# Second block's two norm statistics: every row of squares added on GpSimd, the weighted squares made by ScalarE

## The chip, the cores and the metric
The kernel runs on one core of one Trainium2 chip. The metric is the device time of one launch in microseconds (us), the median of several runs. TensorE, VectorE, ScalarE, GpSimd and SyncE each work through their own instruction list and wait for each other through semaphores. The profile calls them PE (PEld for its weight loads), DVE, ACT, POOL and SP.

## The reference, cut to what matters
Two transformer blocks run one after the other on 256 tokens of width 1024. The first one ends in a norm, the second one begins with one:

```
x = x + 0.5 * ml[8] * swiglu(modulate(rms_norm(x, norm3_g), ml[6], ml[7]), ffn2_w_in, ffn2_w_out)
x = rms_norm(x, final_g)            # end of the first block
h = rms_norm_2(x, norm_mix)         # start of the second block
proj = h @ w_in                     # queries, keys, values, gates, pooled rows
```

With r the reciprocal root of mean(x*x) + eps, the second norm needs the mean of (x * r * final_g) squared. Both means can be had from the x ahead of the first norm: one is the sum of x*x over the 1024 features, the other the sum of (x * final_g) squared. So one statistics step serves both norms.

## The kernel before, in words
Everything is kept with features on the 128 partitions: x is 8 tiles (kc = 0 to 7) of 128 features by 256 tokens. Weights stream in as "units" of 128 x 2048 numbers (1 MB, L378 on SP). ScalarE copies each half of a unit to w_hi in the rounded fp32r format (L524), VectorE forms the rest w_lo = raw - w_hi (L991), and TensorE multiplies high by high, high by low and low by high (L1799 to L1801): for 256 tokens, 8 tiles kc x 2 output tiles x 3 = 48 products in a unit. There are two buffers of each, so unit k+2 is loaded when both halves of w_lo of unit k are made, and it is split when TensorE is through with unit k.

The stage around the change is the end of the first block's second swiglu and the start of the second block. The last four units of the swiglu (`out_parts`, called for i = 0 to 3) give two tiles of x each (m = 0, 2, 4, 6). For each pair the order on VectorE is: add the unit's result to x (L1114), make w_lo of half 1 of the unit two ahead (L991), make x_lo of both tiles (L1161), make w_lo of half 0 of the unit three ahead (L991). The order on ScalarE is: split half 1 of the unit two ahead, x_hi of both tiles (L584), split half 0 of the unit three ahead, squares of both tiles into sq (L588). With i = 1 a table load (L549) stands ahead of this. Each engine goes through this list in order.

TensorE then runs the unit `kcvc` (the second block's first, L2062) on x_hi and x_lo as they come: tile kc waits for that tile's x_lo (`xl_ready`), and the unit's start waits until the swiglu's last but one unit has been added to x (`drained`). Within that unit `mix_ready` puts `mix_stat(kc - 2)`: two products per tile kc of the squares with a two-column operand `sq_gain` (a column of ones and a column of final_g squared), which sum both statistics into ps_a (L2053). The last two tiles' products stand behind the unit. Then come eight products for the gate logits (L2069), and the next unit, inside which at kc = 3 the result of the statistics is spread over partitions (`spread(3, 4)`, L1747).

Behind `stat_done` VectorE makes two variances (L1446 to L1450), ScalarE the root (L782), VectorE half 1 of the w_lo of unit `kcvc` + 2 and the reciprocal (L1054). SP waits for `stat_done` as well, ahead of two 1 MB transfers of late compression weights into sq (L421) and of the later unit loads. GpSimd waits for it ahead of two memsets (L498, L500).

All other norms of the kernel use another way: GpSimd adds the squares of tiles 1 to 5 onto tile 0 (`sums`, L454; `SUMMED` is 6), and TensorE multiplies tiles 6 and 7 and the sum with a column of ones (`stat_rows`, L1730). Each add waits for the one before it.

Of the kernel before, what the change touches and what calls it, by code (L numbers as in the profile page):

```python
# [8 lines left out]
ACT = mybir.ActivationFunctionType  # L9
ALU = mybir.AluOpType  # L10
# [3 lines left out]
P = 128  # L14
D = 1024
KD = D // P
# [3 lines left out]
TT = S // P  # L20
EPS = 1e-6
SUMMED = KD - 2


D_FF = 2816
# [79 lines left out]
def program(nc, a, out):  # L105
    with ExitStack() as ctx:
# [22 lines left out]
        vec = sb("vec", [P, V_END])  # L129
        late_w = sb("late_w", [P, L_END])  # L130
        gg = sb("gg", [P, KD])
        sq_gain = sb("sq_gain", [P, KD, 2])
        sc_pad = sb("sc_pad", [P, KD, MOD_ROWS])
        one_col = sb("one_col", [P, 2, MOD_ROWS])
        turned = sb("turned", [P, MOD_COLS])
# [309 lines left out]
        @block.gpsimd  # L445
        def _(pool):
            def sums(n, width):

                made = n if n < 3 else n - 1
                for kc in range(1, SUMMED):  # L450
                    pool.wait_ge(sq_ready, KD * n + kc + 1)
                    if kc > 1:
                        pool.wait_ge(sq_sums, (SUMMED - 1) * made + kc - 1)
                    pool.tensor_tensor(sq[:, 0, 0:width], sq[:, 0, 0:width], sq[:, kc, 0:width], ALU.add).then_inc(sq_sums, 1)  # L454

            sums(0, NB)
            sums(1, NB)

            for g in range(HKV):
                with pool.Fori(0, 2) as p:  # L460
                    for j in range(2):
                        k = FIRST["conv"] + 4 * g + j
                        if j == 0:
                            pool.wait_ge(drained, FIRST["gates"] + 2 + GROUP * (g + 1))
                        pool.wait_ge(halves_done, 4 * p + 2 * k + 2)
                        pool.tensor_copy(q_cur[:, j, :], q_rows[:, 2 * p + (4 * g + j), :]).then_inc(qcur_ready, 1)
            sums(2, S)

            def pool_group(i):

                w = POOLS[i]
                first = 7 * i
                pool.wait_ge(pool_copied, i // 2 + 1)
                if i:
                    pool.wait_ge(pooled_ready, i)
                pool.tensor_tensor(p_pad[:, PAD:PAD + S], pooled[:, i, :], r_mix, ALU.mult).then_inc(pool_steps, 1)
                pool.wait_ge(pool_steps, first + 1)
                width, step = 1, 0
                bufs = (s1[:, 0, :], s1[:, 1, :])
                while width < w:  # L480
                    dst, lo = bufs[step % 2], 2 * width - 1
                    prev = p_pad if step == 0 else bufs[(step - 1) % 2]
                    ins = pool.tensor_tensor(dst[:, lo:PAD + S], prev[:, lo:PAD + S], prev[:, lo - width:PAD + S - width], ALU.add)
                    step += 1
                    ins.then_inc(pool_steps, 1)
                    pool.wait_ge(pool_steps, first + 1 + step)
                    width *= 2
                sums_w, res = bufs[(step - 1) % 2], bufs[step % 2]
                cnt = cst[:, K_CNT + i * PAD:K_CNT + (i + 1) * PAD]
                pool.tensor_tensor(res[:, 0:PAD], sums_w[:, PAD:2 * PAD], cnt, ALU.mult)  # L490
                pool.tensor_scalar(res[:, PAD:S], sums_w[:, 2 * PAD:PAD + S], 1.0 / w, None, ALU.mult)\
                    .then_inc(pool_steps, 6 - step)
                pool.wait_ge(pool_steps, first + 7)
                pool.tensor_tensor(pooled[:, i, :], res[:, 0:S], p_pad[:, PAD:PAD + S], ALU.subtract).then_inc(pooled_ready, 1)

            pool.wait_ge(sq_sums, 3 * (SUMMED - 1))
            pool.wait_ge(stat_done, 4)
            pool.memset(h_lo[:, 6:8, :].bitcast(F32), 0.0).then_inc(k2_zeroed, 1)  # L498
            pool.wait_ge(k2_zeroed, 1)
            pool.memset(kc_st.bitcast(F32), 0.0).then_inc(k2_zeroed, 1)  # L500
            for r in range(4):
                pool.wait_ge(qk_done, HQ + 2 * r + 1)
                if r == 0:
                    pool.wait_ge(hid_done, 2)
                    pool.wait_ge(rmix_ready, 1)
                    pool.wait_ge(gt_ready, 1)
                pool_group(r)
            sums(4, S)
            sums(5, S)
# [3 lines left out]
        def _(act):  # L513
# [59 lines left out]
                        act.wait_ge(drained, 2 * pr + (k + 3))  # L573
                    act.activation(sq[:, m + t, 0:n], x[:, m + t, 0:n], ACT.Square).then_inc(sq_ready, 1)

            def out_parts(k, m, dst, gain, early):

                split(0, k + 2, 1)
                for t in range(2):
                    if t == 0:  # L580
                        act.wait_ge(first_added, early)
                    else:
                        act.wait_ge(drained, k + 3)
                    act.activation(dst[:, m + t, :], x[:, m + t, 0:S], ACT.Identity, scale=gain(m + t)).then_inc(xh_ready, 1)  # L584
                if m < KD - 2:
                    split(0, k + 3, 0)
                for t in range(2):
                    act.activation(sq[:, m + t, 0:S], x[:, m + t, 0:S], ACT.Square).then_inc(sq_ready, 1)  # L588

            def out_step(pr, k0, i, n, early, last=True, more=True):  # L590

# [68 lines left out]
            def swiglu_wide(base, count):  # L660
                def hidden(pr, k, c, chunks):
                    for m in range(chunks):
                        copy_lo(pr, k + m, m % 2)
                        split(pr, k + m + 2, 1)
                        act.wait_ge(halves_summed, c - count + m + 1)
                        act.activation(s1[:, m % 2, 0:S], s1[:, m % 2, 0:S], ACT.Silu).then_inc(silu_done, 1)
                        act.wait_ge(prod_done, c + m + 1)
                        act.activation(h_hi[:, m, 0:S], t1[:, m % 2, 0:S], ACT.Copy).then_inc(hh_done, 1)
                        split_ahead(pr, k + m)

                split(0, base + 2, 0)
                for s in range(2):
                    hidden(s * 6, base, s * 8 + count, SLABS[0])
                    for i in range(4):
                        split(s * 6, base + SLABS[0] + i + 2, 1)
                        split_ahead(s * 6, base + SLABS[0] + i)
                hidden(0, base + 24, count + 16, SLABS[2])
                for i in range(4):
                    if i == 1:
                        prepare_root()  # L680
                    out_parts(base + 24 + SLABS[2] + i, 2 * i, x_hi[:, :, S:NB], lambda m: gg[:, m:m + 1], 3 + i)


            swiglu(FIRST["ffn1"], 0, NB)
# [286 lines left out]
        def _(dve):  # L971
# [211 lines left out]
                splits(0, 1)  # L1183

            norm_lo(0, 0, NB, modulated(0, 1), 0, between=shift)

            dve.memset(sq_gain[:, :, 0], 1.0)
            dve.tensor_tensor(sq_gain[:, :, 1], vec[:, V_F1:V_F1 + KD], vec[:, V_F1:V_F1 + KD], ALU.mult)

            def swiglu(base, count, n, i):  # L1190
                def gate(m, s):
# [524 lines left out]
        def _(pe):  # L1716
# [2 lines left out]

            def stat_rows(n, tiles, rows, first, last):  # L1720

                made = n if n < 3 else n - 1
                for kc in rows:
                    if kc == 0:
                        pe.wait_ge(sq_sums, (SUMMED - 1) * (made + 1))
                    else:
                        pe.wait_ge(sq_ready, KD * n + kc + 1)
                    for t in range(tiles):

                        ins = pe.matmul(ps_a[:, 3, t:t + 1], sq[:, kc, t * P:(t + 1) * P], ones[:, 0:1],  # L1730
                                        start=(kc == first and t == 0), stop=(kc == last and t == tiles - 1))
                if kc == last:
                    ins.then_inc(stat_done, 1)

            def stat(n, tiles):
                stat_rows(n, tiles, (*range(SUMMED, KD), 0), SUMMED, 0)

            def stat_sums(n, tiles):
                stat_rows(n, tiles, (0,), 0, KD - 1)
# [307 lines left out]

            k = FIRST["kcvc"]

            def mix_stat(kc):  # L2050
                pe.wait_ge(sq_ready, KD * 3 + kc + 1)
                for t in range(TT):
                    ins = pe.matmul(ps_a[:, 3, t:t + TT + 1:TT], sq[:, kc, t * P:(t + 1) * P], sq_gain[:, kc, :],  # L2053
                                    start=(kc == 0 and t == 0), stop=(kc == KD - 1 and t == TT - 1))
                return ins

            def mix_ready(kc):
                pe.wait_ge(xl_ready, 8 * 3 + kc + 1)
                if kc >= 2:
                    mix_stat(kc - 2)  # L2060

            unit(0, k, mix_in, ready=mix_ready)  # L2062
            mix_stat(KD - 2)
            mix_stat(KD - 1).then_inc(stat_done, 1)

            pe.wait_ge(wg_ready, 1)
            for kc in range(KD):
                g = kc % 4
                ins = pe.matmul(ps_a[32 * g:32 * g + 32, 1, 0:S], wg_gain[:, kc * 3 * H2:kc * 3 * H2 + 32], x[:, kc, 0:S],  # L2069
                                start=(kc < 4), stop=(kc >= KD - 4))  # L2070
            ins.then_inc(gt_done, 1)

            def spread_within(kc):
                if kc == 3:
# [350 lines left out]
```

## Time and profile before

| what | value |
|---|---|
| median of 3 runs | 1256.49 us (1254.65 to 1256.58) |
| the profiled execution's own time | 1256.76 us |
| its span in the trace | 1255.0 us |
| granted TensorE clock, mean | 0.996 |
| PE busy | 1239.7 us, 99% |
| DVE busy | 888.6 us, 71% |
| ACT busy | 574.9 us, 46% |
| POOL busy | 55.0 us, 4% |

Times are counted from the start of the span. The stage of the change lies at 866 to 900 us. Matmul records overlap, since TensorE is pipelined: what one costs is the distance from its start to the next one's start. An fp32 product that isn't in the rounded format shows as two records. A "releaser" in square brackets is what ended the idle time ahead of the instruction.

### The profile page before, as it was taken

To read this page: it belongs to the slowest core of one execution; us is meant where nothing else is said; L and a number is where in the kernel's file an instruction comes from. 1 tells how busy PE (TensorE), PEld (TensorE's weight loads), DVE (VectorE), ACT (ScalarE), POOL (GpSimd) and SP (SyncE) were. 2 spreads that over 40 slices of the span, in tenths; PEclk is the share of its full clock that TensorE was granted. 3 is DMA by queue.
4 is the path that set the end of the run, shared out by engine and by line. 5 is a ranking of instruction groups with operands and counts; after the bars stand their busy time and mean duration, and the time that the engine had idled before them with its cause. 6 is when DMAs were issued, how large, how long until landed. Compare 5 with 4: busy or idle time off the path is not lost.

```text
span 1255.0 us, 20607 instructions
## 1 busy us (share of the span) xinstructions
PE 1239.7 (99%) x7778; PEld 1093.1 (87%) x7778; DVE 888.6 (71%) x1395; ACT 574.9 (46%) x880; POOL 55.0 (4%) x65
## 2 busy tenths in 40 slices
PE   8999999999999999999999999999999999999998
PEld 7788888888888799988999888889999999888887
DVE  3887777777754765777666676767769977666765
ACT  3632123221234446554444654556475566554553
POOL 2000000000002000100001000000011301000001
PEclk8999999999999999999999999999999999999999
DMA  9565544455413234422445465544633334455542
GB/s 388 227 237 201 201 184 167 186 201 201 160 62 115 75 144 150 168 101 102 168 167 199 146 245 181 199 174 166 233 135 115 121 131 172 168 187 202 181 168 101
DMA packets 31826, 214.22 MB, mean 171 GB/s; under 512 B 3472, under 2 KB 4752, under 8 KB 7056
## 3 DMA queue, kind: packets, MB, share of 16 engines
q1 hardware_dynamic: 31184, 211.83, 46.0%
q10 hardware_dynamic: 576, 1.48, 0.3%
q8 instruction: 46, 0.75, 0.2%
q14 instruction: 20, 0.16, 0.0%
HBM read 212.24 MB, written 1.05 MB: 170 GB/s over the span
## 4 chain that ended last, share of the span: by engine, by line
PE 95%; DVE 2%; DMA 1%; issue 1%; ACT 0%; SPq 0%; DVEq 0%
PE ps_u L1801 28%; PE ps_u L1799 20%; PE ps_u L1800 19%; PE ps_u L1796 18%; PE ps_a L1718 1%; DMA scr<-in_mods 1%; PE ps_a L2001 1%; PE ps_a L1986 1%; PE ps_a L1764 1%; PE ps_a L1775 1%; PE ps_a L2190 1%; PE ps_a L1753 0%; PE ps_a L1730 0%; PE ps_a L1747 0%; DVE w_lo L991 0%
## 5 line engine op out<-in xcount | busy, mean ns | idle before, releaser
L524 ACT ACTIVATE w_hi<-raw 128x1024 fp32r<-128x1024 f32 x322 | 338.9, 1056 | 313.8 <-PE ps_u L1801 216.0
L991 DVE TENSOR_TENSOR w_lo<-raw,w_hi 128x1024 fp32r<-128x1024 f32 x322 | 393.4, 1223 | 121.0 <-ACT w_hi L524 120.5
L1801 PE MATMUL ps_u<-x_hi,w_lo 128*128 128x256 f32 (+1 forms) x1488 | 460.7, 310 | 0.0
L1799 PE MATMUL ps_u<-x_hi,w_hi 128*128 128x256 f32 (+1 forms) x1136 | 370.7, 326 | 2.5 <-DVE x_lo L1077 1.3
L1800 PE MATMUL ps_u<-x_lo,w_hi 128*128 128x256 f32 (+1 forms) x1072 | 344.2, 321 | 0.0
L1801 PEld LDWEIGHTS ps_u<-x_hi,w_lo 128*128 128x128 f32 x1488 | 282.6, 190 | 15.3
L1801 PE MATMUL ps_u<-h_hi,w_lo 128*128 128x256 f32 (+1 forms) x800 | 244.2, 305 | 0.0
L1799 PEld LDWEIGHTS ps_u<-x_hi,w_hi 128*128 128x128 f32 x1136 | 216.0, 190 | 25.9 <-issue 8.4
L1800 PEld LDWEIGHTS ps_u<-x_lo,w_hi 128*128 128x128 f32 x1072 | 203.9, 190 | 15.3 <-issue 0.5
L1801 PEld LDWEIGHTS ps_u<-h_hi,w_lo 128*128 128x128 f32 x800 | 151.6, 190 | 7.0
L1799 PE MATMUL ps_u<-h_hi,w_hi 128*128 128x256 f32 (+1 forms) x432 | 141.7, 328 | 0.4 <-DVE h_hi L1218 0.4
L1796 PE MATMUL ps_u<-h_hi,w_hi 128*128 128x512 f32 x368 | 129.5, 396 | 0.0
L1796 PE MATMUL ps_u<-x_hi,w_hi 128*128 128x512 f32 x352 | 122.7, 392 | 0.4 <-DVE x_hi L1077 0.4
L1800 PE MATMUL ps_u<-h_lo,w_hi 128*128 128x256 f32 (+1 forms) x368 | 122.9, 334 | 0.0
L1796 PE MATMUL ps_u<-x_lo,w_hi 128*128 128x512 f32 x256 | 90.8, 399 | 0.0
L1799 PEld LDWEIGHTS ps_u<-h_hi,w_hi 128*128 128x128 f32 x432 | 82.1, 190 | 8.4 <-issue 0.8
L1796 PEld LDWEIGHTS ps_u<-h_hi,w_hi 128*128 128x128 f32 x368 | 69.0, 188 | 16.5
L1796 PEld LDWEIGHTS ps_u<-x_hi,w_hi 128*128 128x128 f32 x352 | 65.8, 187 | 15.8 <-issue 1.0
L1800 PEld LDWEIGHTS ps_u<-h_lo,w_hi 128*128 128x128 f32 x368 | 69.9, 190 | 6.9
L1801 PE MATMUL ps_u<-x_lo,w_lo 128*128 128x256 f32 x256 | 71.8, 280 | 0.0
L1024 DVE SCALAR_TENSOR_TENSOR sq<-scr,sc_pad,sq 128x1024 f32<-128x1024 f32 x56 | 68.1, 1279 | 0.0
L1124 DVE TENSOR_TENSOR s<-ps_u,s 128x512 f32<-128x512 f32 x38 | 26.3, 692 | 49.2 <-ACT s L622 48.8
(293 smaller groups left out, 1216.0 us busy)
## 6 DMA issues: line engine op xcount, KB each, us to landing
raw<-in_stream SPq DMA_DIRECT2D x153, 1024.0 KB, 4.8
wide_scr<-in_mods SPq DMA_DIRECT2D x18, 1024.0 KB, 6.9
scr<-in_mods SPq DMA_DIRECT2D x18, 1024.0 KB, 6.9
raw<-in_stream SPq DMA_DIRECT2D x8, 768.0 KB, 4.0
x<-in_tokens SPq DMA_DIRECT2D x2, 1024.0 KB, 6.5
wide_scr<-in_cmp_w SPq DMA_DIRECT2D x8, 256.0 KB, 5.1
sq<-in_cmp_w SPq DMA_DIRECT2D x2, 1024.0 KB, 7.3
out<-x SPq DMA_DIRECT2D x4, 256.0 KB, 2.2
```

The lines of the kernel that those rows point to most:

```text
L524: act.activation(w_hi[:, k % 2, cols], raw[:, k % 2, cols], ACT.Copy).then_inc(h_ready, 1)
L991: dve.tensor_tensor(w_lo[:, k % 2, cols], raw[:, k % 2, cols], w_hi[:, k % 2, cols].bitcast(F32), ALU.subtract).then_inc(l_ready, 1)
L1024: ins = dve.scalar_tensor_tensor(total_v, w[:, kc, :], by, total_v, ALU.mult, ALU.add)
L1124: dve.tensor_tensor(both, ps_u[:, b:b + 2, 0:S], both, ALU.add).then_inc(halves_summed, 1)
L1718: return pe.transpose(dst, src, ident[0:n, 0:n])
L1764: ins = pe.matmul(ps_a[rows, b, 0:MOD_COLS], sc_pad[:, 2 * quarter + kc, :], mod_slots[slot][:, lo:lo + MOD_COLS], start=(quarter == 0 and ...
L1775: ins = pe.matmul(ps_a[rows, MOD_BANKS[c], 0:MOD_COLS], one_col[:, v, :], mod_sums[:, c % 2, v, g * MOD_COLS:(g + 1) * MOD_COLS], start=(v ...
L1796: pe.matmul(ps_u[:, 2 * b + t, :], wh, both, start=(kc == 0), stop=False)
L1799: pe.matmul(dst, wh, xh, start=(kc == 0), stop=False)
L1800: pe.matmul(dst, wh, xl, start=False, stop=False)
L1801: ins = pe.matmul(dst, wl, xh, start=False, stop=(kc == span - 1))
L1986: ins = pe.matmul(ps_a[:, qt, :], q_cur[:, j, qt * P:(qt + 1) * P], k_all[:, g, :], start=True, stop=True)
```

## The change
GpSimd gets a fourth turn, `sums(3, NB)`, over all eight tiles and over 512 columns: columns 0 to 255 hold the squares of x, columns 256 to 511 the squares of x times final_g. ScalarE makes the second half with one more Square per tile, with final_g as its scale. TensorE no longer has `mix_stat`; it multiplies the finished sum by a column of ones, four column blocks of 128 tokens, behind the gate logits' products. `sq_gain` and its two VectorE instructions at the kernel's start go. The table `ADDED` says how many tiles GpSimd adds in each norm, and the semaphore targets follow from it.

```diff
+ADDED = (SUMMED, SUMMED, SUMMED, KD, KD, SUMMED)
@@ gpsimd, sums(n, width)
-                made = n if n < 3 else n - 1
-                for kc in range(1, SUMMED):
+                made = sum(ADDED[0:n]) - n
+                for kc in range(1, ADDED[n]):
                     pool.wait_ge(sq_ready, KD * n + kc + 1)
                     if kc > 1:
-                        pool.wait_ge(sq_sums, (SUMMED - 1) * made + kc - 1)
+                        pool.wait_ge(sq_sums, made + kc - 1)
@@
             sums(2, S)
+            sums(3, NB)
@@ scalar, out_parts(k, m, dst, gain, early, also=None)
                 for t in range(2):
-                    act.activation(sq[:, m + t, 0:S], x[:, m + t, 0:S], ACT.Square).then_inc(sq_ready, 1)
+                    ins = act.activation(sq[:, m + t, 0:S], x[:, m + t, 0:S], ACT.Square)
+                    if also is not None:
+                        ins = act.activation(sq[:, m + t, S:NB], x[:, m + t, 0:S], ACT.Square, scale=also(m + t))
+                    ins.then_inc(sq_ready, 1)
@@ vector
-            dve.memset(sq_gain[:, :, 0], 1.0)
-            dve.tensor_tensor(sq_gain[:, :, 1], vec[:, V_F1:V_F1 + KD], vec[:, V_F1:V_F1 + KD], ALU.mult)
@@ tensor
             def stat(n, tiles):
-                stat_rows(n, tiles, (*range(SUMMED, KD), 0), SUMMED, 0)
+                stat_rows(n, tiles, (0,), 0, 0)
@@
-            def mix_stat(kc): ...
-            def mix_ready(kc): ...
-            unit(0, k, mix_in, ready=mix_ready)
-            mix_stat(KD - 2)
-            mix_stat(KD - 1).then_inc(stat_done, 1)
-
+            unit(0, k, mix_in, ready=normed(3))
             pe.wait_ge(wg_ready, 1)
             for kc in range(KD):
                 ...
             ins.then_inc(gt_done, 1)
+            stat(3, 2 * TT)
```

`stat` is also used by the norm behind the second block's attention (n = 4, `stat(4, 2)` at L2254, between the first two units of the feed-forward stage, around 1068 us). Its entry in `ADDED` is KD as well: there GpSimd now adds all eight tiles of 256 columns, and TensorE multiplies only the sum (two products) where it multiplied tiles 6, 7 and the sum (six).

## Rows read from the trace of the kernel before

**Rows 1.** Page, chain that ended last: shares of the span by engine.
```profile
PE 95%; DVE 2%; DMA 1%; issue 1%; ACT 0%; SPq 0%; DVEq 0%
```

**Rows 2.** Timeline of PE, 879 to 893 us: start, length, line, out<-in, count.
```profile
879.76 0.28 PE L1799 MATMUL ps_u<-x_hi,w_hi 128*128 128x256 f32 x1
...
881.20 0.51 PE L2053 MATMUL ps_a<-sq_gain,sq 128*128 128x2 f32 x4
...
889.04 1.07 PE L2069 MATMUL ps_a<-x,wg_gain 128*32 128x256 f32 x16
890.04 0.39 PE L1799 MATMUL ps_u<-x_hi,w_hi 128*128 128x256 f32 x1
...
892.29 1.05 PE L1747 MATMUL ps_a<-cst,rstd 128*128 128x128 f32 x8
```

**Rows 3.** Timeline of PE at the feed-forward stage's norm (n = 4).
```profile
1068.18 1.39 PE L1730 MATMUL ps_a<-ones,sq 128*128 128x1 f32 x12
1069.44 0.48 PE L1796 MATMUL ps_u<-x_lo,w_hi 128*128 128x512 f32 x1
```

**Rows 4.** Timeline of ACT, 872 to 886 us.
```profile
872.31 0.71 ACT L588 ACTIVATE sq<-x 128x256 f32<-128x256 f32 x2
...
881.82 1.06 ACT L524 ACTIVATE w_hi<-raw 128x1024 fp32r<-128x1024 f32 x1 [1.81 <-DMA raw<-in_stream]
...
884.64 0.91 ACT L584 ACTIVATE x_hi<-x,gg 128x256 fp32r<-128x256 f32 x2 [0.20 <-DVE x L1114]
885.45 0.71 ACT L588 ACTIVATE sq<-x 128x256 f32<-128x256 f32 x2
```

**Rows 5.** Groups by shape, 868 to 890 us: busy us, mean ns of one.
```profile
L584 ACT ACTIVATE x_hi<-x,gg 128x256 fp32r<-128x256 f32 x8 | 3.6, 501 | 1.1 <-DVE x L1114 1.1
...
L588 ACT ACTIVATE sq<-x 128x256 f32<-128x256 f32 x8 | 2.8, 401 | 0.0
```

**Rows 6.** Timeline of DVE, 875 to 892 us.
```profile
875.51 1.23 DVE L991 TENSOR_TENSOR w_lo<-raw,w_hi 128x1024 fp32r<-128x1024 f32 x1 [0.99 <-ACT w_hi L524]
...
878.58 0.87 DVE L1114 SCALAR_TENSOR_TENSOR x<-ps_u,gate_half,x 128x256 f32<-128x256 f32 x2
...
885.18 0.89 DVE L1161 SCALAR_TENSOR_TENSOR x_lo<-x,gg,x_hi 128x256 fp32r<-128x256 f32 x2 [0.19 <-ACT x_hi L584]
...
889.90 0.12 DVE L1446 TENSOR_SCALAR var<-ps_a 128x4 f32<-128x4 f32 x1
...
891.48 0.17 DVE L1054 RECIPROCAL rstd<-root 128x4 f32<-128x4 f32 x1
```

**Rows 7.** Timeline of SP's queue: start of a unit's load.
```profile
876.92 0.33 SPq L378 DMA_DIRECT2D raw<-in_stream  x1
```

**Rows 8.** Timeline of POOL, whole span.
```profile
7.73 6.94 POOL L454 TENSOR_TENSOR sq<-sq 128x512 f32<-128x512 f32 x5 [7.30 <-ACT sq L545]
...
388.65 2.97 POOL L454 TENSOR_TENSOR sq<-sq 128x512 f32<-128x512 f32 x2 [5.59 <-ACT sq L574]
...
940.46 0.74 POOL L494 TENSOR_TENSOR x<-s,p_pad 128x256 f32<-128x256 f32 x1
...
995.65 3.02 POOL L483 TENSOR_TENSOR s<-s 128x269 f32<-128x269 f32 x3
...
1061.36 2.43 POOL L454 TENSOR_TENSOR sq<-sq 128x256 f32<-128x256 f32 x2 [3.33 <-ACT sq L588]
```

**Rows 9.** Timeline of DVE beside three of these.
```profile
387.82 1.21 DVE L991 TENSOR_TENSOR w_lo<-raw,w_hi 128x1024 fp32r<-128x1024 f32 x1
...
940.59 0.89 DVE L1501 TENSOR_TENSOR x<-t 128x256 f32<-128x256 f32 x1
...
996.66 1.41 DVE L991 TENSOR_TENSOR w_lo<-raw,w_hi 128x1024 fp32r<-128x1024 f32 x1
```

**Rows 10.** Timeline of ACT at the norm n = 4.
```profile
1064.49 0.71 ACT L588 ACTIVATE sq<-x 128x256 f32<-128x256 f32 x2
```

**Rows 11.** Stretch: engines' busy time (count), granted PE clock, DMA share, GB/s.
```profile
16.00:18.00 2.00, 0.79 (x8) 0.48 (x11) 0.18 (x1) 0.26 (x1) 0.00 (x0) 0.61 1.02 422
```

More of the change, by code:

```diff
@@ L131, in program @@
         gg = sb("gg", [P, KD])
-        sq_gain = sb("sq_gain", [P, KD, 2])
         sc_pad = sb("sc_pad", [P, KD, MOD_ROWS])
@@ L494, in pool_group @@
                 pool.tensor_tensor(pooled[:, i, :], res[:, 0:S], p_pad[:, PAD:PAD + S], ALU.subtract).then_inc(pooled_ready, 1)
-            pool.wait_ge(sq_sums, 3 * (SUMMED - 1))
+            pool.wait_ge(sq_sums, sum(ADDED[0:4]) - 4)
             pool.wait_ge(stat_done, 4)
@@ L574, in squares, with out_parts @@
                     act.activation(sq[:, m + t, 0:n], x[:, m + t, 0:n], ACT.Square).then_inc(sq_ready, 1)
-            def out_parts(k, m, dst, gain, early):
+            def out_parts(k, m, dst, gain, early, also=None):
                 split(0, k + 2, 1)
@@ L680, in swiglu_wide @@
                         prepare_root()
-                    out_parts(base + 24 + SLABS[2] + i, 2 * i, x_hi[:, :, S:NB], lambda m: gg[:, m:m + 1], 3 + i)
+                    out_parts(base + 24 + SLABS[2] + i, 2 * i, x_hi[:, :, S:NB], lambda m: gg[:, m:m + 1], 3 + i, lambda m: vcol(V_F1, m))
             swiglu(FIRST["ffn1"], 0, NB)
@@ L1720, in stat_rows @@
             def stat_rows(n, tiles, rows, first, last):
-                made = n if n < 3 else n - 1
                 for kc in rows:
                     if kc == 0:
-                        pe.wait_ge(sq_sums, (SUMMED - 1) * (made + 1))
+                        pe.wait_ge(sq_sums, sum(ADDED[0:n + 1]) - (n + 1))
                     else:
@@ L2048, in _ @@
             k = FIRST["kcvc"]
[L2050 to L2060, printed above, removed]
-            unit(0, k, mix_in, ready=mix_ready)
-            mix_stat(KD - 2)
-            mix_stat(KD - 1).then_inc(stat_done, 1)
+            unit(0, k, mix_in, ready=normed(3))
             pe.wait_ge(wg_ready, 1)
```

## The prediction, made blind
> **What bounds the kernel now.** I read the page first. TensorE is busy 99% of the span and makes 95% of the chain that ended last [rows 1], so an edit is worth what it takes from TensorE's own list, less every wait that it puts there. The reader is to see that 71% or 46% busy VectorE and ScalarE have room on average and perhaps none in the stage of the change. So I read next the timelines of that stage, engine by engine: what TensorE spends on the statistics [rows 2], in which order ScalarE and VectorE hand over the last tiles [rows 4, 6], when the next unit's load starts [rows 7]. Last, I looked at what GpSimd's adds cost elsewhere, alone and beside VectorE [rows 8, 9].
>
> **TensorE, first norm (n = 3): saves 3.5, adds 0.84.** The unit `kcvc` starts at 879.76 [rows 2]. Between two `mix_stat` groups six products take 0.72 us, 0.12 each, so its 48 would be through at 885.52; the gate products start at 889.04 [rows 2]. The 16 products of `mix_stat` (32 records) thus cost 3.52 us. The new step has four products, 8 records. Twelve such records cost 1.26 us (1068.18 to 1069.44, [rows 3]), so 8 cost 0.84. Net on TensorE: -2.7 us, if nothing is late.
>
> **TensorE, second norm (n = 4): saves 0.84.** Six products become two, 12 records become 4: 8 x 0.105 = 0.84 us. GpSimd gets two more adds of 256 columns. Its fourth and fifth add take from 1061.36 to 1063.79 with a conflict in them [rows 8], and the squares of tiles 6 and 7 are made from 1064.49 to 1065.2 [rows 10]. Another such pair would be through at 1065.0 + 2.4 = 1067.4, before TensorE asks for the sum at 1068.18: hidden, with 0.8 us to spare. With a second conflict it would be some 0.4 us late, so this term lies between -0.4 and -0.84. I take -0.84.
>
> **ScalarE's second squares: +0.8 us per pair of tiles.** A Square with no operand for its scale takes 0.40 us and two start 0.31 apart (0.71 for two); an activation with a scale per partition takes 0.50 and two start 0.41 apart [rows 4, 5]. I take 0.4 for each of the eight new ones, 0.8 a pair (0.6 if they cost as the plain ones, 1.0 if nothing overlaps). Not all of it is hidden, since the squares stand in the middle of the list:
> - Behind the first pair's squares (872.31) come the table load and the w_hi for which VectorE waits at 875.51 [rows 4, 6]. ScalarE has no idle time in between, so that w_lo starts at 876.3. All of VectorE's list moves with it: the add of the third pair ends at 880.25 instead of 879.45 [rows 6]. The unit `kcvc` needs that bank, and started at 879.76: it starts at 880.3, +0.5 on TensorE.
> - SP's load of the unit after `kcvc` starts right behind that w_lo (876.92, [rows 7]) and lets ScalarE go on at 881.82, 4.9 later [rows 4]. It becomes 877.7 and 882.6.
> - From there ScalarE has w_hi (0.95 to the next start), four squares instead of two (1.5), w_hi (0.95), and then x_hi of the last pair: 886.0, where it was 884.64 [rows 4]. The last x_lo pair, 885.18 before [rows 6], could start at 886.5.
>
> TensorE without `mix_stat` would reach tile 6 at 880.3 + 6 x 0.72 = 884.6. So it waits there in any case: even with ScalarE as before, x_lo of tile 6 comes at 885.65. Part of the old statistics work lay in a time that TensorE would else have waited.
>
> **GpSimd's seven adds.** An add of 512 columns takes 1.27 us alone and the next starts 0.14 later: five in 6.94 [rows 8]. With squares of tiles 4 and 5 at 884.4 and 885.1, of 6 and 7 at 887.6 and 888.3, adds without any disturbance end at 890.3.
>
> They will be disturbed. At 388.65 a pair takes 2.97 instead of 2.68, while a w_lo of VectorE runs until 389.03: the add waited out that instruction [rows 8, 9]. At 940.59 VectorE's 256-column operation takes 0.89, where two of that width take 0.89 together in [rows 6], beside an add that had started 0.13 earlier [rows 8, 9]. So they take turns when VectorE has two operands in SBUF, as w_lo and x_lo do. VectorE's list between 883 and 891 is mostly these. Which of two waiting instructions comes first no row shows. Let them alternate: add 5 takes 886.3 to 887.6; x_lo of tile 6, ready to start at 886.5, takes until 888.0; add 6 until 889.3; x_lo of tile 7 until 889.7; add 7 until 891.0; then the w_lo that was due at 887. TensorE starts tile 6 at 888.05 and tile 7 at 889.75, ends the unit at 890.5, the gate products at 891.5, the new step at 892.3. The next unit started at 890.04 [rows 2]: **+2.3 us**.
>
> Behind it VectorE is one w_lo in arrears. Variances at 889.90, reciprocal at 891.48 to 891.65 [rows 6], 1.75 later; TensorE asked for it at 892.29 [rows 2], 2.25 into its unit. Now VectorE comes to the variances only at 893.3, the reciprocal is there at 895.05, TensorE asks at 894.55: **+0.5**. Together n = 3 gives +2.8.
>
> The Trainium skill, "SBUF — State Buffer", section "SBUF: two separate sides", says of the ports that VectorE and GpSimd share that they are an exclusive lock: whichever starts first has them for its whole instruction and "the other fully blocks". The two cases above agree. The row at 995.65 doesn't: three adds of 269 columns take 3.02 us, at least 0.6 more than three times the 0.74 of a lone 256-column one with gaps, though the second had begun before the w_lo at 996.66, which itself lost only 0.2 of its 1.41 [rows 8, 9]. By the rule the sum stays +2.8; by that row VectorE loses less and the adds more, which is the slow rival below.
>
> **What costs nothing.** The two instructions for `sq_gain` at the start are a few dozen columns (0 to -0.2; I take 0). SP's late weights and the unit loads behind them go out about 3 us later; two 1 MB transfers at 4.9 each [rows 4, 7] have more than a unit and a half of TensorE's time, 9 us and more, before the late weights are read. GpSimd's two memsets move 3 us; the keys that they prepare come several units later. If the late weights had less room, the wait would fall on TensorE one for one. All later work is bound by TensorE, so a delay at 892 is neither made good nor enlarged.
>
> **Sum.** +2.8 - 0.84 = +2.0 us on the profiled execution's 1256.76 us (span 1255.0 and 1.8 around it), which lies 0.3 above the median: **1258.5 us** for a median run. About 0.2%, 2.5 us, is what a measurement of this kernel can tell from no change, so this counts as no change.
>
> **The rivals.**
> - *The adds hardly disturb* (they fall between VectorE's instructions). For it: the pair at 388.65 lost only 0.3. Against: VectorE has little idle time here. Then the adds end at 890.3, the step at 891.15, +1.1 for n = 3, +0.3 in all: 1256.8.
> - *Waits are shorter than I think, TensorE keeps its saving.* ScalarE's squares fall into its waits for loads, x_lo of tile 6 comes at 885.65, the unit ends at 887.15, gate products at 888.15, the step at 889.0: -1.0, with n = 4 -1.9: 1254.6. It needs all seven adds done by 888.15, from squares made at 886.5 at the earliest: against it speaks 1.27 for each of the last adds.
> - *The other side: VectorE keeps the ports, and TensorE's clock falls.* VectorE's x_lo pair and w_lo follow without a gap from 886.45 to 888.5, add 5 runs only then, another w_lo comes between, the last add ends at 893.5, and the next unit starts at 894.35: +4.3, with n = 4 +3.5, 1260.0. TensorE would be through with the gate products at 889.4 and stand idle for over 4 us. Between 16 and 18 us the granted clock fell to 0.61 of full speed on average, that is to 1.2 GHz within the stretch, after small products and waits [rows 11]. If that happens here and 5 us of products run at 1.2 instead of 2.4 GHz, 2.5 us more: 1262.5. It is over the 2.5 us once the last add ends later than 892.55 (then the step is done at 893.4, +3.35, less 0.84), or once the clock falls on top of my own waits.
> - *The change doesn't do what it says*: the final weights' squares are also made by the scaled Square, so the work is the same; I give this nothing.
>
> **How the numbers follow.** My alternating case 0.45 (its own range 1257.2 to 1260, both sides of the bound's edge at 1259.0: a quarter of it counts as slower). The undisturbed adds 0.22, no change. The saving kept 0.08; its -1.9 is just inside the bound, and I give 0.05 to faster. The slow case 0.25. Slower: 0.25 x 0.8 + 0.45 x 0.25, about 0.31; faster 0.05; same 0.64. The range leaves out the fast rival's far end and the clock's: 1255.6 to 1262.0.
>
> **What would show it.** Right: `kcvc` starts 0.3 to 0.6 later against the unit before it; TensorE waits for x_lo of tile 6 by 1.5 to 3.5 us, and the statistics step waits for GpSimd or comes right behind its last add; w_lo, x_lo or adds longer than 1.22, 0.48 and 1.27; at n = 4 no wait, and the next unit 0.84 nearer. Wrong: if the adds all take 1.27, contention is not the term; if ScalarE's list isn't late at 876, the 0.8 per pair isn't; if the next unit starts within 0.5 of 890.0, the waits are overrated; if the granted clock leaves 1.00 near 890, the slow rival has it.

## The result and the profile after

| | before | after |
|---|---|---|
| median | 1256.53 us (6 runs, 1254.65 to 1256.97) | 1264.14 us (6 runs, 1262.60 to 1265.46) |
| profiled execution | 1256.76 us, span 1255.0 | 1264.16 us, span 1262.4 |
| granted clock, mean | 0.996 | 0.994 |

The ratio is 1.0062, with a 95% interval of 1.0049 to 1.0075: slower by 0.6%, where 1258.5 us and a range up to 1262.0 were forecast. A later measurement of the same program, against 35 runs of the kernel before, gave 1.0027 (1.0015 to 1.0038). Why one program has two such results is a question of its own below. The first four experiments ran on one chip (11 on record), this later measurement and all the others on another (6); the chip of the first measurement is not on record. On chip 11 the kernel before had a median of 1256.72 in 30 runs, on chip 6 of 1259.42 in 35.

Where the 7.4 us of the profiled execution lie comes from laying the two lists of TensorE side by side and comparing the distances between the same products. The front of the kernel is 0.5 shorter. The 480 wide products (512 columns) of the second swiglu, whose instructions the change doesn't touch, take 3.1 longer (169.74 for 166.64). From the swiglu's very last product (879.64 before, 882.30 after) to the first product of the compression's hidden layer (`hidden(0)`, L2087 before, L2073 after) it is 22.39 for 17.22, **+5.17**; this is "the stage" from here on. The feed-forward stage, with the norm n = 4, is 0.45 shorter (176.29 for 176.74). The rest agrees within 0.1.

The page's chain has less TensorE in it than the 95% of [rows 1]:
```profile
PE 92%; DVE 3%; DMA 2%; ACT 1%; issue 1%; SPq 0%; DVEq 0%; ACTq 0%
```

Now the timeline of TensorE in the stage. Everything that stands at some time of before is 2.6 later here before the change does anything, because of the longer stage ahead (+3.1) and the shorter front (-0.5); take 2.6 from a time to compare it with [rows 2].
```profile
883.13 0.39 PE L1799 MATMUL ps_u<-x_hi,w_hi 128*128 128x256 f32 x1 [0.55 <-DVE x L1118]
...
890.56 0.38 PE L1799 MATMUL ps_u<-x_hi,w_hi 128*128 128x256 f32 x1 [2.80 <-DVE x_lo L1165]
...
891.99 0.39 PE L1799 MATMUL ps_u<-x_hi,w_hi 128*128 128x256 f32 x1 [0.46 <-DVE x_lo L1165]
...
892.96 1.94 PE L2054 MATMUL ps_a<-x,wg_gain 128*32 128x256 f32 x16
894.83 1.87 PE L1730 MATMUL ps_a<-ones,sq 128*128 128x1 f32 x8
896.56 0.56 PE L1799 MATMUL ps_u<-x_hi,w_hi 128*128 128x256 f32 x1
896.92 0.41 PE L1800 MATMUL ps_u<-x_lo,w_hi 128*128 128x256 f32 x1
897.13 0.41 PE L1801 MATMUL ps_u<-x_hi,w_lo 128*128 128x256 f32 x1
...
900.12 1.05 PE L1747 MATMUL ps_a<-cst,rstd 128*128 128x128 f32 x8
```
Read it from the brackets. TensorE waits at the unit's start, then 2.80 for tile 6 and 0.46 for tile 7. There is no bracket at L1730: GpSimd's sum was never late. Behind the waits every length doubles: the gate products take 1.94 where they took 1.07, and the next unit's products come 0.21 apart and not 0.12. The stretches (start and end, then busy time and count of PE, PEld, DVE, ACT and POOL, granted clock, DMA share, GB/s) give the reason:
```profile
885.00:890.00 5.00, 2.76 (x23) 2.56 (x21) 4.21 (x6) 4.71 (x10) 3.38 (x3) 1.00 0.65 210
890.00:895.00 5.00, 3.98 (x29) 2.30 (x30) 5.00 (x4) 2.93 (x5) 2.79 (x3) 0.77 0.01 2
895.00:900.00 5.00, 5.00 (x25) 5.00 (x26) 2.82 (x8) 0.21 (x1) 1.10 (x2) 0.54 0.89 339
900.00:905.00 5.00, 5.00 (x49) 4.78 (x51) 3.61 (x9) 2.35 (x2) 0.00 (x0) 1.00 1.02 428
```
The clock was at 2.4 GHz, TensorE was busy for only 2.76 of 5 us, and then 1.2 GHz was granted, from 892.7 to 899.6 by the profile's record of it. TensorE has 25 products in the 5 us where the next 5 us hold 49.

VectorE's timeline holds what TensorE waited for:
```profile
884.43 1.91 DVE L1165 SCALAR_TENSOR_TENSOR x_lo<-x,gg,x_hi 128x256 fp32r<-128x256 f32 x2
...
889.14 2.79 DVE L1165 SCALAR_TENSOR_TENSOR x_lo<-x,gg,x_hi 128x256 fp32r<-128x256 f32 x2 [0.68 <-ACT x_hi L585]
891.86 3.43 DVE L995 TENSOR_TENSOR w_lo<-raw,w_hi 128x1024 fp32r<-128x1024 f32 x2
...
896.74 0.16 DVE L1447 TENSOR_SCALAR var<-ps_a 128x4 f32<-128x4 f32 x1 [1.33 <-PE ps_a L1730]
896.93 0.87 DVE L1449 TENSOR_SCALAR var<-var 128x2 f32<-128x2 f32 x1
```
The pair of x_lo that took 0.89 in [rows 6] takes 1.91 and 2.79. The first of these overlaps the end of GpSimd's second line, the other lies inside its third:
```profile
876.72 1.30 POOL L454 TENSOR_TENSOR sq<-sq 128x512 f32<-128x512 f32 x1 [189.52 <-ACT sq L591]
881.64 4.02 POOL L454 TENSOR_TENSOR sq<-sq 128x512 f32<-128x512 f32 x2 [3.62 <-ACT sq L591]
887.13 5.94 POOL L454 TENSOR_TENSOR sq<-sq 128x512 f32<-128x512 f32 x4 [1.47 <-ACT sq L591]
896.82 0.95 POOL L499 MEMSET h_lo<- 128x1024 f32 x1 [3.75 <-PE ps_a L1730]
```
ScalarE's two squares, as groups of the stretch 868 to 893:
```profile
L591 ACT ACTIVATE sq<-x,vec 128x256 f32<-128x256 f32 x8 | 4.0, 496 | 0.0
L589 ACT ACTIVATE sq<-x 128x256 f32<-128x256 f32 x8 | 3.2, 402 | 0.0
```

### The profile page after: what moved, and what is told of

Same layout as the page of the kernel before. It is cut to its first block, busy times and chain, and to the rows that moved or that the text cites. A ratio compares the mean times of both kernels' runs of the same rounds, so it can differ in the third digit from the quotient of the medians.

```text
span 1262.4 us, 20561 instructions
## 1 busy us (share of the span) xinstructions
PE 1243.3 (98%) x7746; PEld 1092.4 (87%) x7746; DVE 894.8 (71%) x1393; ACT 578.2 (46%) x888; POOL 67.8 (5%) x74
## 4 chain that ended last, share of the span: by engine, by line
PE 92%; DVE 3%; DMA 2%; ACT 1%; issue 1%; SPq 0%; DVEq 0%; ACTq 0%
PE ps_u L1801 27%; PE ps_u L1799 19%; PE ps_u L1800 19%; PE ps_u L1796 17%; PE ps_a L1719 1%; DMA scr<-in_mods 1%; DMA raw<-in_stream 1%; PE ps_a L2001 1%; PE ps_a L1986 1%; DVE w_lo L995 1%; PE ps_a L1775 1%; PE ps_a L1764 1%; PE ps_a L1730 1%; PE ps_a L2176 1%; PE ps_a L1753 0%
## 5 line engine op out<-in xcount | busy, mean ns | idle before, releaser
L454 POOL TENSOR_TENSOR sq<-sq 128x512 f32<-128x512 f32 (+1 forms) x34 | 41.8, 1228 | 920.4 <-ACT sq L575 657.9
```

## The experiments

The theory after the result: ScalarE's extra squares make the last x_hi late, GpSimd's adds stretch VectorE's x_lo behind it, TensorE stands still for some 3 us, and its clock falls. Beside that, something that is not the change makes the stages of 512-column products longer or shorter. The rival for the last was that the new or earlier waits on GpSimd do that.

### One norm at a time: n4only and n3only

`n4only` keeps the three new pieces away from n = 3 (`mix_stat`, `sq_gain` and the plain squares are as before). Its table, beside that of the changed kernel:
```diff
-ADDED = (SUMMED, SUMMED, SUMMED, KD, KD, SUMMED)
+ADDED = (SUMMED, SUMMED, SUMMED, 1, KD, SUMMED)
```


> The kernel before with the second norm's half of the change alone: GpSimd adds all eight tiles at n = 4, the first norm stays on TensorE with its 16 products. My theory: 8 records less on TensorE, -0.84 us (12 records took 1.26), the adds hidden; 1255.7 against 1256.5. Rival: this half carries part of the +7.6 us, by conflicts of the two later adds with VectorE's w_lo, or by the slower 512-column products of the swiglu stage (step 236.6 ns instead of 230 between 710 and 866 us): then +2 to +3.

`n3only` is its complement:
```diff
-ADDED = (SUMMED, SUMMED, SUMMED, KD, KD, SUMMED)
+ADDED = (SUMMED, SUMMED, SUMMED, KD, SUMMED, SUMMED)
 def stat(n, tiles):
-    stat_rows(n, tiles, (0,), 0, 0)
+    stat_rows(n, tiles, (0,) if n == 3 else (*range(SUMMED, KD), 0), 0 if n == 3 else SUMMED, 0)
```


> The changed kernel with the second norm as before: the first norm's half of the change alone. My theory: it carries all of the loss, 1264.1 + 0.84 = 1265.0, with the granted clock at 0.5 for some 7 us near 892 and the 512-column products of the swiglu stage at a step of 236.6 ns. Rival (the two halves share the loss): 1262 or less.

`n4only`: 1256.03 us beside 1256.72, ratio 0.9994 (0.9977 to 1.0011), profiled 1253.08. `n3only`: 1263.50, ratio 1.0048 (1.0029 to 1.0067), profiled 1263.50; its stage is 21.40, +4.18, with the clock down for 3.4 us where 7 were expected. All of the loss is in n = 3. (Its ratio is worth 6.0 us and its stage 4.2; the first 480 wide products of this execution are long as well, 169.74.) In TensorE's timeline of `n4only` the twelve records of [rows 3] are four:
```profile
1068.11 0.50 PE L1730 MATMUL ps_a<-ones,sq 128*128 128x1 f32 x4
1068.47 0.48 PE L1796 MATMUL ps_u<-x_lo,w_hi 128*128 128x512 f32 x1
```
From its start to the next product it is 0.36, where it was 1.26: -0.9, and no wait.

### ScalarE's squares alone: actonly

The kernel before, with the second squares made and read by nobody (the diff is cut: `out_parts` also gets the parameter `also`, and this stage's call passes the column of final_g for it):
```diff
 for t in range(2):
-    act.activation(sq[:, m + t, 0:S], x[:, m + t, 0:S], ACT.Square).then_inc(sq_ready, 1)
+    ins = act.activation(sq[:, m + t, 0:S], x[:, m + t, 0:S], ACT.Square)
+    if also is not None:
+        ins = act.activation(sq[:, m + t, S:NB], x[:, m + t, 0:S], ACT.Square, scale=also(m + t))
+    ins.then_inc(sq_ready, 1)
```


> The kernel before plus ScalarE's eight scaled squares, which nobody reads; statistics stay on TensorE. Theory: the squares move VectorE's list by 0.8 at 876 and 1.4 at the last x_lo, but TensorE with its 3.5 us of statistics between the tiles gets to tile 6 only at 885.84, so the wait is under 1 us plus 0.5 at the unit's start: +0.5 to +1.5. Rival: the squares are hidden, under +0.3. The clock stays at 1.00 in both. Swiglu stage: if the slower products come from ScalarE's longer program they show here (236.6 ns); if from GpSimd's waiting, they stay at 230.

1257.83 us beside 1256.72, ratio 1.0013 (1.0001 to 1.0024), profiled stage 18.32, **+1.10**. TensorE's waits in 868 to 905 (what waited, for what: us in total, times, longest):
```profile
PE ps_a L2056 <- DVE x_lo L1164: 0.4, 1, 0.4
PE ps_u L1802 <- DVE x L1117: 0.2, 1, 0.2
```
So ScalarE's list costs only 1.1, in the middle of the +0.5 to +1.5 expected, while `mix_stat` still stands between the tiles: TensorE has that work to do while x_lo is on its way. In the changed kernel the same delay meets an empty TensorE.

### The pace of the wide products, first try: poolwait

```diff
 pool.wait_ge(sq_sums, 3 * (SUMMED - 1))
+pool.wait_ge(sq_ready, KD * 3 + 2)
 pool.wait_ge(stat_done, 4)
```


> The kernel before with one more wait on GpSimd: ahead of its two memsets it waits for the first pair's squares (sq_ready) and then for stat_done, so during the swiglu it stands at the semaphore that the changed kernel's adds wait for, but adds nothing. Theory: which semaphore GpSimd waits for while the products run sets their pace: step 236.6 instead of 230 ns between 710 and 866 us, +3.2 us. Rival: the pace comes from where the loops lie in the program, or from something else in the program: 230 or any other value, and 1256.5 within 0.5.

1256.69 beside 1256.72, ratio 0.9996 (0.9983 to 1.0009), stage 17.22 as before, wide products at 231.6 ns in the first stage. So what GpSimd waits for doesn't fix their pace, and the 3.2 us expected from it are not there. The theory fell. Whether it changes how often they are slow, one profile can't say.

### Is it the clock: fill

The changed kernel, with five products of no use issued ahead of tile 6, so that TensorE is not idle there:
```diff
-unit(0, k, mix_in, ready=normed(3))
+def filled(kc):
+    if kc == 6:
+        keep_busy(5)
+    pe.wait_ge(xl_ready, 8 * 3 + kc + 1)
+
+unit(0, k, mix_in, ready=filled)
```


> The changed kernel with five products of ones by cos1 into an unused bank, which nobody reads, ahead of TensorE's wait for x_lo of tile 6: 2.3 us of work in a wait of 2.8. Theory (the granted clock falls because TensorE stands idle there, and that costs 3.1 us: gate products 1.94 instead of 1.07, statistics 1.87 instead of 0.95, then 1.3 in the next unit): clock 1.00 all through 885 to 905, and 1261.0 in place of 1264.1. Rival (the clock falls from something else, or the loss is all waiting): clock low near 893 as before, 1264 or more.

1261.28 beside 1259.42, ratio 1.0019 (1.0007 to 1.0031), profiled 1256.35. TensorE's timeline, filler first:
```profile
883.87 2.32 PE L1753 MATMUL ps_a<-cst,ones 128*128 128x256 f32 x10
887.01 0.39 PE L1799 MATMUL ps_u<-x_hi,w_hi 128*128 128x256 f32 x1 [0.82 <-DVE x_lo L1165]
...
888.44 0.38 PE L1799 MATMUL ps_u<-x_hi,w_hi 128*128 128x256 f32 x1 [0.45 <-DVE x_lo L1165]
```
The stretch behind it, with the columns of the stretches above:
```profile
890.00:895.00 5.00, 4.68 (x43) 4.13 (x36) 3.85 (x9) 0.72 (x2) 1.11 (x2) 1.00 0.61 218
```
x_lo is as late as before (pairs of 1.91 and 2.79), the idle 2.8 is 0.82, the clock stays at 2.4 GHz throughout, and the stage is 19.76: +2.54 instead of +5.17. The filler does not speed x_lo up; it only keeps the clock. That it does so is shown by more than this execution. Each run's mean granted clock is on record: 0.996 to 0.998 in all twelve of `fill`, as in the kernel before (0.995 to 0.998 in 82 runs), and 0.991 to 0.997 in the twelve of the changed kernel measured beside them (`again`, below), nine of them at 0.995 or less. The times show it less well: the median of `fill` is only 0.5 us below that of `again` (1261.77), the two ratios' intervals overlap, and the 1256.35 of the profiled execution is the lowest of the twelve. So the medians do not show the 3 us expected; by stages the two profiled executions differ by 1.6.

### How much the adds take from VectorE: tinyadds

The changed kernel with adds of one column, so that it leaves the sums out and keeps every wait:
```diff
-sums(3, NB)
+sums(3, 1)
```


> The changed kernel with GpSimd's seven adds of the first norm one column wide instead of 512 (the sums are left out, so the norm's statistic is not the reference's); waits, squares and TensorE's list as in the changed kernel. Theory: the adds cost by holding the ports against VectorE (x_lo 1.91 and 2.79 us for two instead of 0.88, w_lo 3.43 for two): these go back to 0.88 and 2.35, TensorE's wait for tile 6 goes from 2.8 to some 1.7 and the one for tile 7 goes; 1.6 us less waiting, and with less idle time the clock may hold: 1259.4 (with the clock's fall 1262.5). Rival (x_lo is late by ScalarE's squares and the load alone): the wait stays at 2.5 to 2.8, 1263 to 1264.

1258.62 beside 1259.42, ratio 0.9999 (0.9985 to 1.0014), stage 18.52, +1.30. VectorE's last x_lo pair and the way to the reciprocal:
```profile
889.18 0.88 DVE L1165 SCALAR_TENSOR_TENSOR x_lo<-x,gg,x_hi 128x256 fp32r<-128x256 f32 x2 [0.68 <-ACT x_hi L585]
...
893.43 0.17 DVE L1447 TENSOR_SCALAR var<-ps_a 128x4 f32<-128x4 f32 x1
893.63 0.86 DVE L1449 TENSOR_SCALAR var<-var 128x2 f32<-128x2 f32 x1
...
895.74 0.17 DVE L1058 RECIPROCAL rstd<-root 128x4 f32<-128x4 f32 x1
```
TensorE at tile 6:
```profile
889.72 0.38 PE L1799 MATMUL ps_u<-x_hi,w_hi 128*128 128x256 f32 x1 [2.28 <-DVE x_lo L1165]
```
With nothing to take turns with, the pair is at 0.88 again and tile 7 has no wait. Tile 6 still waits 2.3, more than the 1.7 expected: what is left is ScalarE's delay and the removed statistics (how the two share it is not shown). The clock held in this execution, after 2.3 of idle time ahead of tile 6; with 2.8 to 3.0 there it fell in each of the four that show it (the changed kernel twice, `n3only`, `sixadds`). But 2.3 is not safe: two of the other runs of `tinyadds` have a mean granted clock of 0.993 and 0.994, lower than any of the 82 runs of the kernel before.

### Fewer adds, more on TensorE: sixadds

```diff
-ADDED = (SUMMED, SUMMED, SUMMED, KD, KD, SUMMED)
+ADDED = (SUMMED, SUMMED, SUMMED, SUMMED, KD, SUMMED)
 def stat(n, tiles):
-    stat_rows(n, tiles, (0,), 0, 0)
+    stat_rows(n, tiles, (*range(SUMMED, KD), 0) if n == 3 else (0,), SUMMED if n == 3 else 0, 0)
```


> The changed kernel with the first norm's sum over six tiles instead of eight: GpSimd's adds 6 and 7 go, TensorE multiplies tiles 6 and 7 as well, 12 products (24 records, 2.5 us) instead of 4 (0.84). Theory: adds 6 and 7 ran beside the last x_lo and the two w_lo behind it; without them the second x_lo and w_lo are not held, 0.5 us less waiting, 1.7 more products, but the clock falls all the same since the wait for tile 6 stays 2.8: 1264.5 to 1266. Rival: conflicts at the end are the main loss, 1262 or less.

1262.46 beside 1259.42, ratio 1.0037 (1.0017 to 1.0057), below the 1264.5 to 1266 expected; profiled 1269.14 with a stage of 27.59, +10.4. TensorE waited 3.0 for tile 6 (until 890.5), and the clock fell for 17.1 us, here from 889.5 on, with the wait not yet over:
```profile
890.00:895.00 5.00, 4.50 (x28) 3.23 (x28) 3.27 (x6) 2.88 (x5) 0.17 (x1) 0.50 0.38 103
895.00:900.00 5.00, 5.00 (x27) 4.77 (x23) 0.00 (x0) 0.00 (x0) 0.00 (x0) 0.50 0.25 107
```
Its runs lie in two groups, 1258.3 to 1263 and 1267.8 to 1269.1, and only one of the second is profiled. The mean granted clock tells them apart: 0.990 to 0.992 in the four of the second group, 0.994 to 0.996 in the six of the first. So the second group is that of the long fall.

### The changed kernel once more: again

No edit.

> The changed kernel once more, unedited, to have more runs of it beside the others on one chip. If its six runs of 1262.6 to 1265.5 are typical: 1264.1. If the pace of the 512-column products (230 or 236 ns in the profiled executions, which differs from kernel to kernel and once changed within a run) is drawn anew in each execution, and the profiled one had the slow pace in both stages: median 1262.5, runs from 1259 to 1267.

1261.77 beside 1259.42, ratio 1.0027 (1.0015 to 1.0038), profiled 1261.33. Stage 21.33, +4.11, with the waits of the first profile (3.3 for x_lo, 0.5 at the start) and a fall of the clock half as long, 3.4 us:
```profile
890.00:895.00 5.00, 4.19 (x28) 2.73 (x28) 5.00 (x4) 2.74 (x5) 2.58 (x3) 0.66 0.01 2
```
So the waits belong to the kernel, and the length of the fall to the execution; two of the twelve runs, with a mean clock of 0.997, seem to have had none.

### The kernel before, three times, and n = 4 alone: base_a to base_c, n4_again

The three of base are the kernel before, unedited; `n4_again` is `n4only`, unedited.

> The kernel before, unedited, for a second profiled execution. Theory (the pace of the 512-column products is drawn anew in each execution): the two stages of such products, 710 to 866 us and 1100 to 1240 us, run at about 230 or about 236.5 ns from start to start, in combinations that differ between executions of this one program, and the time is near 1253.4, 1256.5 or 1259.8 us as none, one or both of them are slow. Rival (the pace belongs to the program): 230 in the first stage and 236.7 in the second again, as in the first profile of this kernel.

> The kernel before once more, unedited, a third profiled execution. As for the last: by the theory of a draw at least one of the two new executions shows another combination of paces than 230 and 236.7; by the rival both show that one, and 1256.5 us.

> The kernel before, a fourth profiled execution. In each of the four, time less the extra of the slow stages (3.3 us each by the earlier profiles) should be 1253.2 within 0.7 us if the pace is all that moves this kernel's time.

> The candidate: the change at the second norm (n = 4) alone, once more, to narrow its interval. Forecast -0.84 us, a ratio of 0.9993, from eight records of 0.105 us; with this kernel's executions spread over 6 us the interval will probably be some 0.0015 wide to each side and not exclude 1. Rival (something else is lost elsewhere by the two later adds): 1.0000 or over.

| kernel before | first wide stage | second wide stage | time |
|---|---|---|---|
| first profile | 166.64 | 176.74 | 1256.76 |
| base_a | 166.64 | 176.81 | 1256.27 |
| base_b | 169.73 | 174.08 | 1256.63 |
| base_c | 166.63 | 176.82 | 1256.21 |

The wide stages are TensorE's times from the first to the last of 480 (second swiglu) and 496 (feed-forward stage) wide products. One and the same program has either the one long or the other. It can be read in any profile, from the mean length of such a product (groups by shape, 720 to 860 us). In the first profile of before:
```profile
L1796 PE MATMUL ps_u<-x_hi,w_hi 128*128 128x512 f32 x277 | 96.2, 391 | 0.0
```
In `base_b`, the same program, in the same stretch (the changed kernel's row is the same to the last digit):
```profile
L1796 PE MATMUL ps_u<-x_hi,w_hi 128*128 128x512 f32 x269 | 95.2, 399 | 0.0
```
From start to start it is 230.0 ns where the mean is 391 and 236.7 where it is 399: 480 x 6.7 = 3.2 us, and 3.1 measured. The rival of a pace that belongs to the program falls. What does not fall is that the program changes the odds: the first wide stage is long in five of the six profiled executions in which GpSimd has its fourth turn (the changed kernel twice, `n3only`, `tinyadds`, `sixadds`; short in `fill`), and in one of the eight without it (`base_b`). That it explains the whole spread holds for these four (1256.2 to 1256.8, one long stage in each); the kernel before's other runs have no trace. They lie around 1253.5, 1256.5 and 1259.7, as none, one or two long stages would give, and `n4only`'s profile, with both short, shows 1253.08.

`n4_again`: 1255.64, ratio 0.9983 (0.9969 to 0.9997). It says more than the 0.8 us that the stages show (below), because the runs of the kernel before beside it had a median of 1259.16: nine of those 17 lie above 1259, as two long wide stages would give, and of these twelve only two lie above 1258. Whether that is the draw or the edit is open. The profiled one, with one long stage of 176.01, is 0.73 to 0.81 shorter there than before's three of that kind, and its time is 1255.83 where those have 1256.21 to 1256.76. With `n4only` that makes a gain of 0.8 us, 0.06%: the only version here that is faster than the kernel before, and by less than the noise of one measurement of its time.

## Why the prediction was wrong, point by point

- **The step that failed** is the choice of the likeliest case: a long wait of TensorE for tile 6 was forecast and the fall of the clock was given to the slow rival alone, with 0.25. The main sum, +2.8 for n = 3, thus has the term of the clock at nothing, and the range leaves it out. In the profiled execution the fall costs 3.0 us: 0.87 in the gate products (1.87 from start to start for 1.00), 0.82 in the statistics (1.73 for the 0.91 of `fill`), and 1.31 in the next unit (spread at 3.56 for 2.25). Without these the stage would be +2.2. In `fill`, whose clock held, it is +2.5, a wait of 0.3 for the reciprocal among it (the filler was through at 886.2, ahead of x_lo at 887.0, and adds nothing). In [rows 11] the price stood in plain sight, and the row was tied to the wrong condition: no jam of the adds is needed, the forecast's own gap at tile 6 (3.4, from 884.6 to 888.05) was longer than the one that took the clock. The clock is about half of the miss; the long wide stage, on which the prediction has no word, is the other half. With only one of the two, the 1264.1 would have been some 1261.1 and inside the range.
- **ScalarE's list: right.** A scaled square adds 0.40 from start to start (a plain one has 0.30), 0.8 a pair. The unit `kcvc` starts late by 0.55 of idle time, 0.7 by distance, for +0.5. The last x_lo pair could start at 886.5 by the forecast and does at 889.14 - 2.6 = 886.5.
- **Turns on the ports: right.** Tile 6 was forecast for 888.05 and starts at 890.56 - 2.6 = 888.0; tile 7 for 889.75, and 889.4; gate products for 890.5, and 890.4; last add 891.0, and 893.07 - 2.6 = 890.5. In the last line GpSimd gave up little (5.94 for four adds that take 5.5 undisturbed) and VectorE much (1.9 in the last x_lo pair, 1.1 in the two w_lo behind); in the line before it, GpSimd gave up 1.3 (4.02 for two that take 2.7) and VectorE 1.0. So the rival in which VectorE keeps the ports is wrong in its mechanism, though its clock came true; its price, +4.3 without the clock's fall, is twice the +2.2 measured. The Trainium skill's exclusive lock ("SBUF — State Buffer", section "SBUF: two separate sides") fits these rows. It also fits the three adds of [rows 8] that the prediction held against it: that row is a sum of three, and by the groups of the trace of before, shape by shape, only the last and narrowest of them is long:
```profile
L483 POOL TENSOR_TENSOR s<-s 128x269 f32<-128x269 f32 x3 | 1.9, 636 | 0.2
L483 POOL TENSOR_TENSOR s<-s 128x257 f32<-128x257 f32 x1 | 1.6, 1602 | 0.1
```
  It runs from 997.08 to 998.68, and the w_lo of [rows 9] until 998.07: it waited out the w_lo, as the lock has it. By `tinyadds` and `fill` the turns cost 2.54 - 1.30 = 1.2 us of the stage while the clock holds.
- **Removed and added work on TensorE: right in amount, wrong in worth.** The eight records cost 0.91 where the clock is high (`tinyadds`, `fill`), for 0.84: one comes to 0.11 and not 0.105. The 3.5 us of `mix_stat` were called partly a filler of waits; `actonly` shows how much: with it in place ScalarE's delay costs 1.1, and TensorE's longest wait is 0.4.
- **The reciprocal: nearly right in size, wrong in cause.** 0.3 was seen in `n3only`, `fill`, `tinyadds` and the second profile of the changed kernel, for +0.5 forecast. VectorE is not a w_lo in arrears: in the changed kernel it waits 1.33 for the statistics (1.03 in the second profile; only in `fill` does it come to them straight from a w_lo, 0.2 after GpSimd's memset has begun). The memset of GpSimd, costed at nothing, now runs beside the variances and makes L1449 0.87 long (0.17 in the kernel before); in `tinyadds` the way from L1447 to the reciprocal is 2.31 where [rows 6] has 1.58. In the first profile of the changed kernel the slow clock hid it.
- **n = 4: right**, -0.8 to -0.9 for -0.84, hidden adds included (1072.83 to 1075.25, asked for at 1076.04). The profiled changed kernel kept only 0.45 of it; most of the rest goes between the 62nd and 71st wide product, beside a wait of 0.22 for h_hi. The second profile has such a wait (0.18) at the same product and loses there too; `sixadds` and `n4_again`, with the same adds at n = 4, have none. What makes it stays open.
- **"A delay is neither made good nor enlarged": half right.** Behind the stage nothing moves (within 0.1), but inside it the delay bred 3.0 more.
- **The measurement.** Of the 7.4 in the profiled pair, 3.1 is the long first wide stage. The change need not be its cause, since `base_b` has it without the change; that it makes it no likelier is not shown (five of six against one of eight, above). Without it, the change is +5.2 - 0.45 = +4.7 in that execution and +4.1 - 0.8 = +3.3 in the second, and the ratio of 1.0027 is 3.4 us. The two ratios' intervals don't overlap. That the first six changed runs had mostly two long stages and before's six one would do it; only one of the six has a trace, and it has two. The second ratio is set against a kernel before that was itself 2.9 us slower (1259.42 for 1256.53). The bound of 0.2% for what can be told from no change was too small for a kernel that moves in steps of 3 us.

## What to carry to other kernels

Work that an engine does while it would wait anyway is free, and taking it away frees nothing; on TensorE it can cost twice, because the gap that it leaves can take the clock. So whoever forecasts a wait of some 3 us on a TensorE that is busy all the time must put the lower clock into the main sum (a mean clock per run shows whether it fell, where there is no trace), and look whether a few idle products, a later tile order, or less work ahead of the late operand closes the gap. And where a kernel's runs fall into steps, compare stage by stage between profiles before a difference of that size is put down to an edit, and count over several profiles how often each step comes with the edit and without it.

## What was not expected of the hardware

- Products of 512 columns run at 230.0 or at 236.7 ns from start to start, mostly for a whole stage of some 170 us, with the granted clock at 1.00 in both. (231.9 and 236.0 occur as well and go with the same two stage times: 166.63 in `base_c`, 169.75 in `tinyadds`.) It differs between executions of one program. In `poolwait` it changed within a stage, from 230 to 236 at 1136.7 us, behind a wait of TensorE of 0.5; in `again` it changed twice, once behind a wait of 0.18 and once behind none. What draws it is open.
- Behind an idle time of 2.8 to 3.0 us on TensorE (with 0.2 to 0.5 more at the unit's start, and 0.5 at tile 7 in three of the four), 1.2 GHz was granted for 3.4 us twice, for 6.8 once and for 17.1 once. Behind one of 2.3 it was not in the profiled execution; the mean clocks of that kernel's other runs suggest that it was in some.
- Beside a memset on GpSimd of 0.95 us, a two-column instruction of VectorE took 0.86 or 0.87 us instead of 0.17, in five profiles (the changed kernel twice, `n3only`, `tinyadds`, `sixadds`).
